# Idle products of 128x256 on TensorE behind steps of the two recurrences in the layers

## The chip, the cores and the metric

The kernel runs as one program on one core of a Trainium2 chip. TensorE (PE) multiplies matrices, VectorE (DVE), ScalarE (ACT) and GpSimd (POOL) do the element-wise work, and SyncE (SP) issues the transfers. The time is device microseconds of one launch. TensorE's clock has two levels, 2.4 and 1.2 GHz; the profile shows the granted clock as a share of the higher one, so 1.00 and 0.50.

## The reference, cut to what matters

The model is two blocks. The first has two layers of feed-forward, mixer, feed-forward. Its mixer runs three mechanisms on the same projected rows (sequence 512): a sparse attention that keeps 128 keys per query, chosen by a small indexer (`dsa`), an RWKV-7 recurrence (`rwkv`) and a gated delta rule (`delta`). The second block has a forgetting attention with a gated linear attention, a cross attention and a mixture of experts. The change touches the two recurrences of the first block alone. In the reference they are:

```
# rwkv7_scan, per step
sa = jnp.einsum('bhij,bhj->bhi', S, at)
S = S * wt[:, :, None, :] + sa[..., None] * bt[:, :, None, :] + vt[..., None] * kt[:, :, None, :]
y = jnp.einsum('bhij,bhj->bhi', S, rt)

# chunk_gated_delta_rule, per chunk
v_new = uc - jnp.einsum('bhck,bhkv->bhcv', wc, S)
o = jnp.einsum('bhck,bhkv->bhcv', qc * jnp.exp(gc)[..., None], S) + jnp.einsum('bhcs,bhsv->bhcv', ac, v_new)
S = S * jnp.exp(g_last)[..., None, None] + jnp.einsum('bhck,bhcv->bhkv', kc * jnp.exp(g_last[..., None] - gc)[..., None], v_new)
```

## The kernel before, in words

Both recurrences are computed in four chunks of 128 tokens, q = 0 to 3, four heads of width 64 each. Every chunk is a chain of small fp32 products with a copy out of PSUM between them.

- `rwkv_pe` (strand `r`) works in banks 0 and 1. For each q it makes the masked scores (AK, RB, RK; line 1107 through `scores`), then `wv` (1204, 1205), `sa` (1211: four products of 128x64), `y` (1223 to 1225) and `state` (1234, 1235). DVE copies between them: `wv` at 1428, `sa` at 1432, the state at 1439. Behind the last chunk come the means (1240: two products of 128x512).
- `delta_pe` (strand `d`) works in banks 2, 3 and 4 (`R.D4` is bank 4; its `B[0]` is bank 2). For each q: `rest` (1573), `vn` (1579), `delta_y` (1590, 1591) and `delta_state` (1601). DVE reads them at 1781, at 1788 and 1789, and at 1797.
- `dsa_pe` (strand `s`) works in banks 5 to 7: the indexer's products (1984) with ACT's relu (2027) and DVE's sum (2091), then DVE's choice of the keys, sixteen rounds of MAX8 and MATCH_REPLACE8 (2101, 2103), and then the attention: scores (1864), transposes (1873), values (1882).

Each engine's program is written out by `in_turns(TURNS, ...)`: a strand is a Python generator, each `yield` ends a step, and `TURNS` is a fixed list of letters that says whose step comes next. All four engines use the same list. Nothing is reordered at run time: on each engine the instructions run in the order written, and one that waits for a semaphore holds up all behind it.

A product signals its reader by `.then_inc` on the last instruction of its step, so a product written behind that one does not delay the signal; it stands ahead of whatever comes next on PE. An fp32 product is recorded as two matmuls in the profile, so a count of x8 is four products. The shapes in the rows are the stationary tile, and then output and input.

The kernel has idle products already, in `norm_pe`, whose result nobody reads:

```
for _ in range(2):
    e.matmul(bank[first][:, :], ones, C("cmask"), start=True, stop=True)
```

`ones` is a 128x128 constant of ones, and `C("cmask")` a constant of 128x512, of which the first 384 columns are zero.

Of the kernel before, what the change touches and what calls it, by code (L numbers as in the profile page):

```python
# [16 lines left out]
NT = SEQ // P  # L17
# [147 lines left out]
def build(nc, x_in, mem_in, const_in, w1_in, w2_in, y_out):  # L165
    with ExitStack() as ctx:
# [56 lines left out]
        def C(name, n=None):  # L223
            a, w = CONST[name]
            return const[:, a:a + w] if n is None else const[:, a + n * P:a + (n + 1) * P]
# [19 lines left out]
        ident, ones, bones = C("ident"), C("ones"), C("bones")  # L245
# [542 lines left out]

        def head_sum(stat, c, t):
            return stat[:, 2 * (c * NT + t):2 * (c * NT + t) + 2]

# [330 lines left out]
        def rwkv_pe(e, R):  # L1124
            l, B, W = R.l, R.B, R.W
# [4 lines left out]
            for c in range(2):  # L1130
                for n, (lo, hi) in enumerate(LORA):
                    if 3 * c + n >= 2:
                        e.wait_ge(*act.at("lora", l, 3 * c + n - 2))
                    e.matmul(B[(3 * c + n) % 2][:, :], up[lo:hi, c * P:(c + 1) * P], R.lora[lo:hi, :], start=True,
                             stop=True).then_inc(*pe.step(("up", l, 3 * c + n)))
# [54 lines left out]
            for q in range(NT):  # L1190
                for n, (lhs, rhs) in enumerate(((R.Kt, R.At), (R.Bt, R.Rt), (R.Kt, R.Rt))):
                    if n:
                        e.wait_ge(*dve.at(("AK", "RB")[n - 1], l, q))
                    else:
                        e.wait_ge(*(dve.at("state_raw", l, q - 1) if q else dve.at("T", tag, 6, NT - 1)))
                    scores(e, lhs, rhs, q, B).then_inc(*pe.step((("AK", "RB", "RK")[n], l, q)))
                    yield
                e.wait_ge(*dve.at("RK", l, q))
                e.wait_ge(*dve.at("scaled", l, q))
                for half in range(2):  # L1200
                    part = half_of(half)
                    for c in range(2):
                        h, o = 2 * half + c, B[half][:, c * HD:(c + 1) * HD]
                        e.matmul(o, R.At[part, cols_of(c, q)], R.scaled[part, c, :], start=True, stop=False)
                        made = e.matmul(o, R.AK[:, h, :], R.v_tok[:, q, c * P + half * HD:c * P + (half + 1) * HD],
                                        start=False, stop=True)
                    made.then_inc(*pe.step(("wv", l, q, half)))
                yield
                e.wait_ge(*dve.at("wv", l, q))
                for h in range(4):  # L1210
                    made = e.matmul(B[0][:, h * HD:(h + 1) * HD], R.Tt[:, q, h, :], R.wv[:, h, :], start=True, stop=True)
                made.then_inc(*pe.step(("sa", l, q)))
                yield
                e.wait_ge(*dve.at("sa", l, q))

                def vs(h):
                    return R.v_tok[:, q, (h % 2) * P + (h // 2) * HD:(h % 2) * P + (h // 2 + 1) * HD]

                for half in range(2):
                    part = half_of(half)  # L1220
                    for c in range(2):
                        h, o = 2 * half + c, B[half][part, c * P:(c + 1) * P]
                        e.matmul(o, R.scaled[part, c, :], R.Rt[part, cols_of(c, q)], start=True, stop=False)
                        e.matmul(o, R.sa[:, h, :], R.RB[:, h, :], start=False, stop=False)
                        made = e.matmul(o, vs(h), R.RK[:, h, :], start=False, stop=True)
                    made.then_inc(*pe.step(("y", l, q, half)))
                yield
                for half in range(2):
                    part = half_of(half)
                    e.wait_ge(*act.at("y", l, q, half))  # L1230
                    for c in range(2):
                        h, o = 2 * half + c, B[half][part, c * HD:(c + 1) * HD]
                        hs = slice(c * P + half * HD, c * P + (half + 1) * HD)
                        e.matmul(o, R.b_tok[:, q, hs], R.sa[:, h, :], start=True, stop=False)
                        made = e.matmul(o, R.k_tok[:, q, hs], vs(h), start=False, stop=True)
                    made.then_inc(*pe.step(("state", l, q, half)))
                yield
# [252 lines left out]
        def delta_pe(e, R):  # L1490
# [73 lines left out]
            for q in range(NT):  # L1564
                if q:
                    e.wait_ge(*dve.at("state", l, q - 1))
                else:
                    e.wait_ge(*dve.at("state0", l))
                    e.wait_ge(*act.at("q_decay", l, 1))
                for half in range(2):  # L1570
                    part = half_of(half)
                    for c in range(2):
                        made = e.matmul(B[half][:, c * HD:(c + 1) * HD], kf[part, cols_of(c, q)], R.state[part, c, :],
                                        start=True, stop=True)
                    made.then_inc(*pe.step(("rest", l, q, half)))
                yield
                e.wait_ge(*dve.at("rest", l, q))
                for h in range(4):
                    made = e.matmul(R.D4[:, h * HD:(h + 1) * HD], R.Tt[:, q, h, :], R.rest[:, h, :], start=True,
                                    stop=True)  # L1580
                made.then_inc(*pe.step(("vn", l, q)))
                yield
                e.wait_ge(*dve.at("vn", l, q))
                if q == 0:
                    e.wait_ge(*dve.at("q_decay", l, 1))
                for half in range(2):
                    part = half_of(half)
                    for c in range(2):
                        h, o = 2 * half + c, B[half][part, c * P:(c + 1) * P]
                        e.matmul(o, R.state[part, c, :], qf[part, cols_of(c, q)], start=True, stop=False)  # L1590
                        made = e.matmul(o, R.vn[:, h, :], R.Xt[:, q, h, :], start=False, stop=True)
                    made.then_inc(*pe.step(("delta_y", l, q, half)))
                yield
                e.wait_ge(*dve.at("vs", l, q))
                for half in range(2):
                    part = half_of(half)
                    e.wait_ge(*act.at("delta_y", l, q, half))
                    for c in range(2):
                        h, o = 2 * half + c, B[half][part, c * HD:(c + 1) * HD]
                        hs = slice(c * P + half * HD, c * P + (half + 1) * HD)  # L1600
                        made = e.matmul(o, R.k_tok[:, q, hs], R.vs[:, h, :], start=True, stop=True)
                    made.then_inc(*pe.step(("delta_state", l, q, half)))
                yield
            yield from heads_pe(e, ("o", l), W, R.stat, B, [dve.at("state", l, NT - 1)])
            yield
# [1866 lines left out]
```

## Time and profile before

| | |
|---|---|
| median of 3 runs | 3742.98 us (3742.59 to 3748.95) |
| profiled execution: its own time, its span | 3745.36 us, 3743.6 us |
| PE, PEld, DVE, ACT, POOL busy | 93%, 75%, 51%, 37%, 12% |
| mean granted clock | 0.941 |
| HBM traffic over the span | 110 GB/s |

The span is from the first to the last instruction of one profiled execution; the time of that execution is 1.76 us longer. Busy shares are averages over stages with quite different limits. In the chain that ended last, the costliest lines lie in the experts at the end of the program (L2925, 10% of the span). The mixers of the two layers lie between about 385 and 945 us and between about 1730 and 2290 us; their last parts, where the recurrences run beside the sparse attention, are from 780 and from 2125 us on.

### The profile page before, as it was taken

Reading aid. Unit: us, or ns where it says so; the run is one execution under the profiler, and the core shown is the slowest. Engines: PE = TensorE matmul, PEld = TensorE weight load, DVE = VectorE, ACT = ScalarE, POOL = GpSimd, SP = SyncE. Lnnn points to the kernel's source line nnn. Section 1 sums busy time; section 2 is a strip of 40 time slices with the busy share of each in tenths; the row PEclk is TensorE's granted clock in tenths of the full one; section 3 lists DMA queues with packets and bytes.
Section 4 is the critical chain, followed back from the end, with each engine's and each line's share of the span. In section 5 each row is a group of like instructions: output and inputs, shape, how many; then the busy total and the mean of one; then the engine's idle time right before and its main releaser. Section 6 shows DMA issues by size and latency. Waiting matters only on the chain. (4 is left out here: it accounts for less than half of the span.)

```text
span 3743.6 us, 43164 instructions
## 1 busy us (share of the span) xinstructions
PE 3494.3 (93%) x17900; PEld 2809.5 (75%) x17900; DVE 1913.4 (51%) x2897; ACT 1397.2 (37%) x1940; POOL 436.0 (12%) x217
## 2 busy tenths in 40 slices
PE   8999996998999999999997989999999998699995
PEld 6888786875788888887786856888777665578884
DVE  4343444675443444343626764434335333389995
ACT  3222443642321232123444524312244333277772
POOL 1000332000000000002321000000131000122222
PEclk9999998996999999999998969999998989799997
DMA  4443210000223222222100002222221211499994
GB/s 172 148 139 114 79 68 1 1 23 23 90 90 108 90 100 92 100 92 88 71 24 1 24 1 79 90 103 90 102 90 46 79 46 45 184 362 409 407 408 150
DMA packets 65986, 414.61 MB, mean 111 GB/s; under 512 B 6912, under 2 KB 11136, under 8 KB 22272
## 3 DMA queue, kind: packets, MB, share of 16 engines
q1 hardware_dynamic: 63488, 403.46, 28.8%
q0 software_dynamic: 2304, 8.39, 0.6%
q8 instruction: 142, 2.33, 0.3%
q14 instruction: 52, 0.43, 0.0%
HBM read 375.13 MB, written 36.70 MB: 110 GB/s over the span
## 5 line engine op out<-in xcount | busy, mean ns | idle before, releaser
L344 DVE TENSOR_TENSOR w_lo<-ring,w_hi 128x2048 fp32r<-128x2048 f32 x146 | 334.4, 2292 | 869.0 <-ACT w_hi L340 869.0
L340 ACT ACTIVATE w_hi<-ring 128x2048 fp32r<-128x2048 f32 x146 | 280.1, 1920 | 1001.9 <-PE bank L469 584.6
L469 PE MATMUL bank<-x_hi,w_lo 128*128 128x512 f32 x1344 | 533.5, 397 | 0.0
L469 PE MATMUL bank<-x_hi,w_hi 128*128 128x512 f32 x1344 | 527.3, 392 | 0.0
L469 PE MATMUL bank<-x_lo,w_hi 128*128 128x512 f32 x1344 | 524.2, 390 | 0.0
L469 PEld LDWEIGHTS bank<-x_lo,w_hi 128*128 128x128 f32 x1344 | 252.3, 188 | 62.2
L469 PEld LDWEIGHTS bank<-x_hi,w_lo 128*128 128x128 f32 x1344 | 252.3, 188 | 58.0
L469 PEld LDWEIGHTS bank<-x_hi,w_hi 128*128 128x128 f32 x1344 | 252.3, 188 | 54.5
L513 PE MATMUL bank<-h_hi,w_hi 128*128 128x512 f32 x704 | 274.0, 389 | 0.0
L513 PE MATMUL bank<-h_hi,w_lo 128*128 128x512 f32 x704 | 274.0, 389 | 0.0
L513 PE MATMUL bank<-h_lo,w_hi 128*128 128x512 f32 x704 | 273.8, 389 | 0.0
L372 POOL TENSOR_TENSOR tmp<-tmp 128x512 f32<-128x512 f32 x54 | 76.0, 1407 | 1182.9 <-ACT tmp L365 1176.4
L2906 ACT ACTIVATE e_hi<-arena 128x2048 fp32r<-128x2048 f32 x92 | 176.3, 1916 | 24.0 <-PE bank L2925 21.2
L2911 DVE TENSOR_TENSOR e_lo<-ring,e_hi 128x2048 fp32r<-128x2048 f32 x45 | 150.0, 3333 | 44.0 <-ACT e_hi L2906 44.0
L2911 DVE TENSOR_TENSOR e_lo<-arena,e_hi 128x2048 fp32r<-128x2048 f32 x70 | 157.6, 2276 | 6.1 <-ACT e_hi L2906 6.1
L513 PEld LDWEIGHTS bank<-h_hi,w_hi 128*128 128x128 f32 x704 | 132.2, 188 | 27.5
L513 PEld LDWEIGHTS bank<-h_lo,w_hi 128*128 128x128 f32 x704 | 132.2, 188 | 27.5
L513 PEld LDWEIGHTS bank<-h_hi,w_lo 128*128 128x128 f32 x704 | 132.2, 188 | 27.5
L703 PE MATMUL bank<-x_hi,ring_r 128*128 128x512 f32 x352 | 139.8, 397 | 0.0
L2916 POOL TENSOR_TENSOR e_lo<-arena,e_hi 128x2048 fp32r<-128x2048 f32 x22 | 101.8, 4625 | 318.3 <-ACT e_hi L2906 318.3
L998 POOL TENSOR_TENSOR ring_r<-ring,high 128x1024 fp32r<-128x1024 f32 x44 | 110.4, 2532 | 225.7 <-ACT high L990 225.7
L998 POOL TENSOR_TENSOR ring_r<-ring,first 128x1024 fp32r<-128x1024 f32 x6 | 14.3, 2405 | 1045.7 <-ACT first L990 1045.7
(562 smaller groups left out, 6988.2 us busy)
## 6 DMA issues: line engine op xcount, KB each, us to landing
ring<-slots SPq DMA_DIRECT2D x238, 1024.0 KB, 4.8
arena<-slots SPq DMA_DIRECT2D x92, 1024.0 KB, 8.4
x_rows<-v_first SPq DMA_DIRECT2D x23, 512.0 KB, 6.7
xn<-x_rows SPq DMA_DIRECT2D x23, 512.0 KB, 8.3
y_rows<-xn SPq DMA_DIRECT2D x23, 512.0 KB, 8.8
x_aside<-xT SPq DMA_DIRECT2D x3, 2048.0 KB, 6.3
xT<-x_aside SPq DMA_DIRECT2D x3, 2048.0 KB, 9.0
xT<-x_t SPq DMA_DIRECT2D x2, 1024.0 KB, 10.4
```

Of the source, the lines that this page charges most:

```text
L340: e.activation(w_hi[:, k % 2, :], ring[:, k % RING, :], ACT.Copy).then_inc(*act.step(("hi", k)))
L344: e.tensor_tensor(w_lo[:, k % 2, :], ring[:, k % RING, :], w_hi[:, k % 2, :].bitcast(F32), ALU.subtract).then_inc(*dve.step(("slot", k)))
L372: e.tensor_tensor(SUM[:, :], SUM[:, :], squares[i][:, :], ALU.add).then_inc(*pool.step(("sum", tag, i)))
L469: made = e.matmul(bank[b + f][:, :], w.rearrange("p (k n) -> p k n", k=KC)[:, c, f * P:(f + 1) * P], (x_hi, x_lo)[part][:, c, :], start=c ...
L513: made = e.matmul(bank[d][:, :], w.rearrange("p (f n) -> p f n", f=2)[:, f, d * P:(d + 1) * P], rows[part][:, 2 * n + f, :], start=n == 0 ...
L703: made = e.matmul(out, w[:, c0:c0 + P], x, start=i == 0 and m == 0, stop=i == KC - 1 and m == 2)
L998: e.tensor_tensor(half_slot(ring_r[:, k % RING, :], half), raw, half_slot(high_of(N, n), half).bitcast(F32), ALU.subtract).then_inc(*pool. ...
L2906: e.activation(e_hi[m % W_BUFS][:, :], e_ring[m % E_RING], ACT.Copy).then_inc(*act.step(("expert_hi", m)))
L2911: e.tensor_tensor(e_lo[m % W_BUFS][:, :], e_ring[m % E_RING], e_hi[m % W_BUFS][:, :].bitcast(F32), ALU.subtract).then_inc(*dve.step(("expe ...
L2916: e.tensor_tensor(e_lo[m % W_BUFS][:, :], e_ring[m % E_RING], e_hi[m % W_BUFS][:, :].bitcast(F32), ALU.subtract).then_inc(*pool.step(("exp ...
```

## The change: one product behind some steps

A helper is added, and is called behind four kinds of step. With q from 0 to 3 that makes 2 products (`sa`), 3 (`rest`), 4 (`vn`) and 3 (`delta_state`), so 12 in each layer and 24 in all. None has a wait or a signal of its own. Each writes 256 columns of a bank that its strand has read and that the strand's next use overwrites.

```diff
+        def idle_product(e, b):
+
+            e.matmul(b[:, 0:256], ones, C("cmask")[:, 0:256], start=True, stop=True)
+
@@ rwkv_pe
                 made.then_inc(*pe.step(("sa", l, q)))
+                if q >= 2:
+                    idle_product(e, B[1])
                 yield
@@ delta_pe
                     made.then_inc(*pe.step(("rest", l, q, half)))
+                if q:
+                    idle_product(e, R.D4)
                 yield
@@
                 made.then_inc(*pe.step(("vn", l, q)))
+                idle_product(e, B[0])
                 yield
@@
                     made.then_inc(*pe.step(("delta_state", l, q, half)))
+                if q < NT - 1:
+                    idle_product(e, R.D4)
                 yield
```

The order of all other instructions is the same on every engine. Line numbers move: a line of the strands stands 4 to 11 lines further down in the kernel after (1984 becomes 1995); L793 is the new product. Three places on PE follow, each of one layer.

The first is chunk q = 1 of `delta`, where `rest` (second half), the indexer's products and `vn` alternate. Before:

```order
L1573 MATMUL bank3<-arena 128x64 x2
L1984 MATMUL bank5<-arena 128x512
L1984 MATMUL bank6<-arena 128x512
L1579 MATMUL bank4<-arena,xn 128x64 x4
L1984 MATMUL bank5<-arena 128x512
L1984 MATMUL bank6<-arena 128x512
```

After, in the same place:

```order
L1579 MATMUL bank3<-arena 128x64 x2
L793 MATMUL bank4<-const 128x256
L1995 MATMUL bank5<-arena 128x512
L1995 MATMUL bank6<-arena 128x512
L1587 MATMUL bank4<-arena,xn 128x64 x4
L793 MATMUL bank2<-const 128x256
L1995 MATMUL bank5<-arena 128x512
L1995 MATMUL bank6<-arena 128x512
```

Two products stand ahead of the first and of the second pair of the indexer's products.

The second is chunk q = 2 of `rwkv`: the end of `wv`, `sa`, and the start of `y`. Before:

```order
L1204 MATMUL bank1<-arena,xT 128x64
L1205 MATMUL bank1<-arena 128x64
L1211 MATMUL bank0<-arena 128x64 x4
L1223 MATMUL bank0<-xT,arena 64x128
L1224 MATMUL bank0<-arena 64x128
```

After:

```order
L1208 MATMUL bank1<-arena,xT 128x64
L1209 MATMUL bank1<-arena 128x64
L1215 MATMUL bank0<-arena 128x64 x4
L793 MATMUL bank1<-const 128x256
L1229 MATMUL bank0<-xT,arena 64x128
L1230 MATMUL bank0<-arena 64x128
```

One product stands between `sa` and `y`; there is none ahead of `sa`, in `wv`.

The third is behind chunk q = 1 of `delta`, where its state step, the scores of the attention (L1864) and `rest` of q = 2 follow each other. Before:

```order
L1601 MATMUL bank3<-arena,xT 64x64 x2
L1864 MATMUL bank5<-arena 128x512
L1573 MATMUL bank2<-arena 128x64 x2
L1573 MATMUL bank3<-arena 128x64 x2
L1864 MATMUL bank5<-arena 128x512
```

After:

```order
L1610 MATMUL bank3<-arena,xT 64x64 x2
L793 MATMUL bank4<-const 128x256
L1875 MATMUL bank5<-arena 128x512
L1579 MATMUL bank2<-arena 128x64 x2
L1579 MATMUL bank3<-arena 128x64 x2
L793 MATMUL bank4<-const 128x256
L1875 MATMUL bank5<-arena 128x512
```

Each of the two scores has a product in front of it.

## Rows read from the trace of the kernel before

**Rows 1.** The page of the profile: span, section 1, and the granted clock by slice.

```profile
span 3743.6 us, 43164 instructions
...
PE 3494.3 (93%) x17900; PEld 2809.5 (75%) x17900; DVE 1913.4 (51%) x2897; ACT 1397.2 (37%) x1940; POOL 436.0 (12%) x217
...
PEclk9999998996999999999998969999998989799997
```

**Rows 2.** Windows view, both layers' slow stretches and the end of the first.

```profile
842.60:900.60 58.00, 47.90 (x193) 30.59 (x194) 40.24 (x99) 6.63 (x15) 0.00 (x0) 0.50 0.00 0
2187.40:2245.40 58.00, 47.90 (x194) 30.59 (x193) 40.24 (x99) 6.63 (x15) 0.00 (x0) 0.50 0.00 0
...
885.60:900.50 14.90, 14.85 (x46) 7.76 (x46) 6.94 (x26) 4.37 (x9) 0.00 (x0) 0.50 0.00 0
```

**Rows 3.** Windows view, two microseconds each, around the clock's fall and rise.

```profile
840.00:842.00 2.00, 2.00 (x12) 1.43 (x10) 1.69 (x3) 1.00 (x2) 0.00 (x0) 1.00 0.00 0
842.00:844.00 2.00, 1.62 (x9) 1.29 (x8) 1.18 (x4) 0.00 (x0) 0.00 (x0) 0.65 0.01 4
...
848.00:850.00 2.00, 2.00 (x9) 1.20 (x8) 1.93 (x4) 0.09 (x1) 0.00 (x0) 0.50 0.00 0
...
900.00:902.00 2.00, 2.00 (x9) 0.81 (x8) 0.69 (x1) 0.00 (x0) 0.00 (x0) 0.84 0.00 0
```

**Rows 4.** Timeline of PE, layer 0 (start, length, line, tiles, shape, count, idle before).

```profile
834.07 1.10 PE L1579 MATMUL bank<-arena,xn 128*128 128x64 f32 x8
835.10 1.23 PE L1984 MATMUL bank<-arena 64*128 64x512 f32 x4
...
839.68 0.33 PE L1204 MATMUL bank<-arena,xT 64*128 64x64 f32 x2
...
843.45 1.97 PE L1211 MATMUL bank<-arena 128*128 128x64 f32 x8 [0.38 <-DVE arena L1428]
846.49 0.68 PE L1223 MATMUL bank<-xT,arena 64*64 64x128 f32 x2 [1.07 <-DVE arena L1432]
...
876.83 0.68 PE L1223 MATMUL bank<-xT,arena 64*64 64x128 f32 x2 [1.40 <-DVE arena L1432]
...
885.65 2.07 PE L1864 MATMUL bank<-arena 64*128 64x512 f32 x2 [1.69 <-DVE arena L2124]
...
888.51 2.07 PE L1864 MATMUL bank<-arena 64*128 64x512 f32 x2
...
892.04 1.97 PE L1579 MATMUL bank<-arena,xn 128*128 128x64 f32 x8
...
896.80 3.78 PE L1240 MATMUL bank<-arena,const 128*128 128x512 f32 x4
```

**Rows 5.** Timeline of PE, first span: where the clock came back at 791.

```profile
786.39 3.73 PE L850 MATMUL bank<-ring 128*128 128x128 f32 x16
789.91 1.78 PE L859 MATMUL bank<-xn,tmp 128*128 128x128 f32 x8
```

**Rows 6.** Timeline of PE: the kernel's own idle products of 128x512.

```profile
383.39 1.45 PE L405 MATMUL bank<-const 128*128 128x512 f32 x3
```

**Rows 7.** Source view of that line: least, median and greatest length in ns.

```profile
L405 PE MATMUL bank<-const x12: 592/592/592, 383.4 to 2705.6; 128*128 128x512 f32 x12
```

**Rows 8.** Timeline of PE behind the slow stretch, layer 0.

```profile
907.38 0.66 PE L1873 MATMUL bank<-const,arena 128*128 128x128 f32 x4 [0.28 <-ACT arena L1923]
```

**Rows 9.** Timeline of DVE in the slow stretch, layer 0.

```profile
846.01 0.42 DVE L1432 COPY arena<-bank 128x256 f32<-128x256 f32 x1
...
853.32 0.28 DVE L1439 TENSOR_TENSOR arena<-arena,bank 64x128 f32<-64x128 f32 x1 [2.34 <-PE bank L1235]
854.82 0.29 DVE L1439 TENSOR_TENSOR arena<-arena,bank 64x128 f32<-64x128 f32 x1 [1.21 <-PE bank L1235]
...
860.93 0.76 DVE L1113 TENSOR_TENSOR arena<-bank,const 128x256 f32<-128x256 f32 x2 [3.85 <-PE bank L1107]
...
896.91 0.69 DVE L1908 CUSTOM_DVE_ANT_0 arena<-bank,arena 128x512 f32<-128x512 f32 x1 [2.03 <-PE bank L1864]
```

## The prediction, made before the result was known

> **What bounds the kernel now.** I read the page first. PE is busy for 93% of the span, but the granted clock by slice is not 9 everywhere: it dips where the mixers of the layers are [rows 1]. Since the change adds work to PE and removes none, it can only pay through that clock, so the next view was the windows view around the recurrences. Its columns are the stretch, its length, then busy time of PE, PE's weight loads, DVE, ACT and POOL, and then the granted clock. In each layer there is a stretch of 58 us, 842.6 to 900.6 and 2187.4 to 2245.4, in which the clock is at 0.50 throughout (1.2 GHz). The two are alike to the hundredth, so I work on the first and double it [rows 2].
>
> Then the finer windows, to see what PE did before the clock fell and before it rose [rows 3]. It fell at 842.6, and from 840 to 842 PE was busy for 2.00 of 2.00 us. So no idle time stands directly ahead of the fall. The timeline says what filled these microseconds: `wv`, sixteen products of only 64 columns, from 839.68 on [rows 4]. The clock stayed low through `y`, where PE is busy without a break (848 to 850), and it came back at 900.6. Ahead of that stand four full matmuls of 128x512 that took 3.78 us from 896.80 on. The same was seen at 791, where `wv` and `sa` of q = 1 were followed by 16 and 8 matmuls of 128x128, 3.73 and 1.78 us long, in a row [rows 5]. Both times about four to five microseconds of work on the full 128x128 tile brought the clock back.
>
> Last, who waits in the slow stretch. Up to 885 DVE is the busier side. It chooses the keys, and PE waits for it before `y` of q = 2 (1.07 us), before `y` of q = 3 (1.40) and before the first scores (1.69) [rows 4]. But DVE also waits for PE, 2.34, 1.21 and 3.85 us around `state` and `delta_y` of the slow clock [rows 9]. From 885.6 to 900.5 PE is busy for 14.85 of 14.90 us and the others wait for it [rows 2, 9].
>
> **The change part by part.** It adds 24 products of 128x256, 12 in each layer. The price of one is from the kernel's own idle products. Three recorded matmuls of 128x512 take 1.45 us, and one alone 592 ns, so they start (1450 - 592) / 2 = 429 ns apart [rows 6, 7]. A product of 512 columns is two such matmuls, so one of 256 columns costs 0.43 us at full clock. At half clock four such matmuls took 3.78 us, 0.94 each, and a product of 256 columns costs 0.94 [rows 4]. In the order of the layer:
>
> 1. Four at full clock ahead of the fall: behind `vn` and `delta_state` of q = 0, and behind `rest` and `vn` of q = 1. PE has no gap there: `vn` at 834.07 plus 1.10 us meets the indexer's products at 835.10 [rows 4]. The last two stand ahead of indexer products, from which ACT's relu, DVE's sum and the whole choice of keys hang in a chain, so a delay of PE goes straight into DVE. On the path: 4 x 0.43 = 1.72 us.
> 2. Behind `sa` of q = 2, behind `sa` of q = 3, and behind `delta_state` of q = 1: these fill the waits of 1.07, 1.40 and 1.69 us, each longer than 0.94 [rows 4]. What hides them is DVE's choice of keys; DVE reaches its copy of `sa` at 846.01 straight from that work, with no wait for PE [rows 9]. Cost 0. Without the cover they would cost 3 x 0.94.
> 3. Behind `rest` and `vn` of q = 2, at half clock, in the stretch where PE has no gap. Behind the first stand the scores of 888.51, and DVE and ACT wait for those; behind the second stand the transposes and then the scores for which DVE waits 2.03 us [rows 4, 9]. On the path: 2 x 0.94 = 1.88 us.
> 4. Behind `delta_state` of q = 2 and `rest` and `vn` of q = 3, at full clock again. One wait of PE of 0.28 us behind `rest` takes up a part [rows 8]: 3 x 0.43 - 0.28 = 1.01 us.
>
> That is 1.72 + 1.88 + 1.01 = 4.6 us a layer and 9.2 us for both, if the clock stays as it is.
>
> The products are not seen in their places before, so both sides. From below each costs nothing, if its time disappears in a wait further on that the trace puts down elsewhere: 0 us. From above each also pays a weight load that nothing covers. A product of 64 columns in `vn` takes 1.10 / 4 = 0.27 us at full clock and 1.97 / 4 = 0.49 at half, nearly all of it such overhead [rows 4]; seven times 0.27 and twice 0.49 add 2.9 us a layer, so 15 us in all. I take the middle value, because the kernel's own idle products run 429 ns apart with their weight loads hidden.
>
> Now the clock. Does it still fall at `wv` of q = 2? I say yes. No product is inserted in `wv` or ahead of `sa`; the nearest one before stands ahead of the indexer products of 835.10, 4.6 us before `wv` starts [rows 4], and the nearest one after comes when `sa` is done. Between them the row of small products is what it was. Does it come back sooner? One product gives 0.94 us of full-tile work, where the two rises of this trace had 3.78 and 5.5 us of it in a row [rows 4, 5]. The closest the change comes to that is behind `vn` of q = 2: a product, transposes, scores of 64 rows, and then the same four matmuls as before. So I leave the clock's pattern as it is. The moment of the fall can shift by a microsecond or two against the program, since everything ahead of it runs 1.7 us later; at half against full clock that is worth below 1 us a layer with either sign.
>
> [...] The fall at 842.6 with PE busy throughout speaks against busy time alone as the measure.
>
> The sum against the profiled execution is 3745.36 + 9.2 = 3754.6. That execution is 2.4 us above the median of the runs shown, so against the median it is 3742.98 + 9.2 = 3752.2. I predict 3752.
>
> **The rivals.** A, the clock holds: from `sa` of q = 2 on it stays at 1.00, in both layers. For it: five of the twelve products stand within the slow stretch, three of them in the very waits of PE. Against: the fall with PE busy, and nothing added in `wv`. What it gives: of the 7.4 us that DVE waits (2.34 + 1.21 + 3.85) I take half, 3.7. In the 14.9 us at the end, `vn` goes from 1.97 to 1.10 us, a ratio of 0.56, so 6.6 us are saved. That is 10.3 a layer. The products cost 9 x 0.43 - 0.28 = 3.6 then. Net -6.7 a layer, 3742.98 - 13.4 = 3729.6. It decides from the point where the windows around 846 show 1.00. This is the rival on the other side, faster than before.
>
> B, the clock comes back early, behind `delta_state` of q = 1. There `y` and both state steps end in a dense run, and the new product lengthens it by 0.94 us ahead of the scores of 885.65. Then the last 14.9 us run at full clock: -6.6, products 3.6, net -3.0 a layer and 3737.0 for both. In one layer alone: -3.0 + 4.6, so 3744.6. For it: this is the densest run with a product behind it. Against: `y` and the state step use tiles of half the rows or half the columns, and at half clock they never brought a rise by themselves [rows 3].
>
> C, the products are hidden in places where I put them on the path, because ACT and DVE set the pace of the attention between 832 and 842 and behind 901. Half the price of parts 1 and 4: 1.4 us a layer less, and 3749.5; if part 3 is hidden too, 3745.7. For it: PE does wait for ACT there, 0.28 us [rows 8]. Against: these waits are far shorter than a product.
>
> D, the change doesn't do what it says: the moving operand is all zeros, and such products may not count as activity at all. The time is that of the forecast, 3752; only the windows with products in them would tell it apart.
>
> **How the numbers follow.** The forecast with D: 0.62. C: 0.14. B: 0.12, shared between one and both layers. A: 0.12. About 0.2%, 7.5 us, is what a measurement of this kernel can tell from no change. Of the forecast's 0.62 some 0.45 lies above 3750.5, and 0.17 between that and the median, since the bounds 0 and 15 us and the shift of the moments at which the clock changes spread it. C is within 0.2%. Of B half a case is: one layer is within 0.2%, both layers are just within it or below, 0.05 faster. A is faster. So faster 0.17, same 0.38, slower 0.45. The forecast's own range is 3746 to 3758. The range for 8 in 10 takes in C and B and leaves out A below, and above it stops at the upper bound of the price: 3737 to 3758.
>
> **What would show it.** Right: 48 matmul records of the new line, 214 ns of streaming each at full clock; a clock of 0.50 still from about 844 to 905, longer by the two products of part 3; the waits before `y` of q = 2 and q = 3 gone or nearly gone with `y` no later against DVE's copy; the indexer's first products 1.3 us later than before and its second pair 1.7. Wrong: a clock of 1.00 anywhere between 846 and 896 (A or B); a length from 832 to the end of the mixer that has grown by less than 3 us with the same clock (C); a slow stretch in a stage that the change doesn't touch.

## The result and the profile after

The changed kernel took 3758.75 us (median of 6 runs), 14.9 us more than before beside it (3743.89): a ratio of 1.0044, with a 95% interval of 1.0028 to 1.0061. Measured again in one session with experiments, it took 3758.06 against 3744.87, 1.0036 [1.0023, 1.0049]. It is slower, as predicted, but by 13 to 15 us and not by 9.

The page of the kernel after, against [rows 1]:

```profile
span 3757.8 us, 43260 instructions
...
PE 3513.2 (93%) x17948; PEld 2821.4 (75%) x17948; DVE 1914.0 (51%) x2897; ACT 1397.2 (37%) x1940; POOL 435.4 (12%) x217
...
PEclk9999998996999999999998978999998988699997
```

48 matmuls more (an fp32 product of 256 columns is two), 18.9 us more of busy PE, and the same picture of the clock but for single slices. The windows view after, in answer to [rows 2, 3]:

```profile
845.20:847.20 2.00, 1.61 (x11) 1.36 (x10) 1.30 (x5) 0.00 (x0) 0.00 (x0) 0.89 0.01 4
847.20:905.20 58.00, 51.07 (x197) 31.69 (x196) 39.21 (x97) 6.64 (x15) 0.00 (x0) 0.50 0.00 1
2202.30:2260.30 58.00, 51.13 (x197) 31.80 (x196) 39.25 (x97) 6.64 (x15) 0.00 (x0) 0.50 0.00 1
```

The mean of 0.89 in the first row puts the fall at 846.8, 4.1 us later than before; the second came 14.4 us later (2201.85 against 2187.47). The clock stayed at 0.50 for the same 58.0 us. (The windows shown here and below, from other traces than that of before, start 0.1 to 0.7 us behind the fall.) PE is busy for 51.1 of them in place of 47.9: three gaps were filled or shortened, and the length of the slow stretch did not change. The timeline of PE after, at the places of [rows 4]; L793 is the new product:

```profile
824.78 0.65 PE L793 MATMUL bank<-const 128*128 128x256 f32 x2
825.27 0.49 PE L1884 MATMUL bank<-const,arena 128*128 128x128 f32 x3
...
835.02 0.70 PE L793 MATMUL bank<-const 128*128 128x256 f32 x2
835.65 1.13 PE L1995 MATMUL bank<-arena 64*128 64x512 f32 x4
...
847.92 1.17 PE L793 MATMUL bank<-const 128*128 128x256 f32 x2
849.46 0.69 PE L1229 MATMUL bank<-xT,arena 64*64 64x128 f32 x2 [0.38 <-DVE arena L1438]
...
888.63 2.07 PE L1875 MATMUL bank<-arena 64*128 64x512 f32 x2 [0.53 <-DVE arena L2135]
...
891.55 1.22 PE L793 MATMUL bank<-const 128*128 128x256 f32 x2
892.70 2.07 PE L1875 MATMUL bank<-arena 64*128 64x512 f32 x2
...
897.99 1.17 PE L793 MATMUL bank<-const 128*128 128x256 f32 x2
898.95 1.06 PE L1884 MATMUL bank<-const,arena 128*128 128x128 f32 x4
```

The price of a product is the distance from its start to the next start: 825.27 - 824.78 = 0.49 us where a full tile follows, 835.65 - 835.02 = 0.63 where a tile of 64 rows follows (0.59 at 837.65, behind `vn` of q = 1); at half clock 898.95 - 897.99 = 0.96 and 892.70 - 891.55 = 1.15. The wait before `y` of q = 2 shrank from 1.07 to 0.38 us, that before the scores from 1.69 to 0.53.

Where did the 14.2 us between the two spans arise? DVE passes four marks that both programs have: its work behind `state` of q = 1 in each layer (just ahead of the first product), and its first splitting of weights behind each mixer. Before:

```profile
823.03 0.59 DVE L1439 TENSOR_TENSOR arena<-arena,bank 64x128 f32<-64x128 f32 x2
...
961.97 2.29 DVE L344 TENSOR_TENSOR w_lo<-ring,w_hi 128x2048 fp32r<-128x2048 f32 x1 [12.68 <-ACT w_hi L340]
...
2167.88 0.60 DVE L1439 TENSOR_TENSOR arena<-arena,bank 64x128 f32<-64x128 f32 x2
...
2306.80 2.29 DVE L344 TENSOR_TENSOR w_lo<-ring,w_hi 128x2048 fp32r<-128x2048 f32 x1 [12.65 <-ACT w_hi L340]
```

And after:

```profile
823.73 0.59 DVE L1445 TENSOR_TENSOR arena<-arena,bank 64x128 f32<-64x128 f32 x2
...
967.87 2.29 DVE L344 TENSOR_TENSOR w_lo<-ring,w_hi 128x2048 fp32r<-128x2048 f32 x1 [11.19 <-ACT w_hi L340]
...
2178.88 0.59 DVE L1445 TENSOR_TENSOR arena<-arena,bank 64x128 f32<-64x128 f32 x2
...
2322.95 2.29 DVE L344 TENSOR_TENSOR w_lo<-ring,w_hi 128x2048 fp32r<-128x2048 f32 x1 [11.16 <-ACT w_hi L340]
```

By differences, the first layer's part took 138.94 us and now 144.14, the second's 138.92 and now 144.07: 5.2 a layer. But the stretch between them, in which no product stands, went from 1205.91 to 1211.01: 5.1 us more. I call these three lengths the parts of a trace; before they are 138.9, 1205.9, 138.9. The rest of the 14.2 us lies outside them: 0.7 us more ahead of the first mark, and 2.0 less behind the last one (3757.8 - 2322.95 against 3743.6 - 2306.80), in the second block.

The extra in the middle is the clock. The windows view after shows it at half speed at places of the program where the trace of before has it at full speed, with PE busy throughout:

```profile
1758.50:1761.90 3.40, 3.40 (x10) 2.62 (x10) 0.00 (x0) 1.40 (x2) 0.20 (x1) 0.55 0.40 164
1901.90:1905.30 3.40, 3.40 (x19) 3.40 (x19) 0.25 (x1) 2.00 (x2) 1.39 (x1) 0.56 0.10 39
1942.40:1945.80 3.40, 3.40 (x32) 3.16 (x32) 1.77 (x3) 0.00 (x0) 0.00 (x0) 0.50 0.00 0
```

The third of these falls has a counterpart before, but in another place of the program, some 5 us of work earlier, where DVE is idle for 2.98 us until a result of POOL:

```profile
1928.10:1931.50 3.40, 3.40 (x17) 3.40 (x17) 0.42 (x2) 0.86 (x2) 3.01 (x2) 0.50 0.00 0
```

By the starts of the same instructions on DVE in both traces, 1.6, 1.6 and 1.7 us are lost at the three places: 4.9 of the 5.1.

### The profile page after: what moved, and what is told of

It is laid out like the page before. It is cut to its first block and busy times, and to the rows that moved or that the text cites. A ratio compares the mean times of both kernels' runs of the same rounds, so it can differ in the third digit from the quotient of the medians.

```text
span 3757.8 us, 43260 instructions
## 1 busy us (share of the span) xinstructions
PE 3513.2 (93%) x17948; PEld 2821.4 (75%) x17948; DVE 1914.0 (51%) x2897; ACT 1397.2 (37%) x1940; POOL 435.4 (12%) x217
## 5 line engine op out<-in xcount | busy, mean ns | idle before, releaser
L1002 POOL TENSOR_TENSOR ring_r<-ring,first 128x1024 fp32r<-128x1024 f32 x6 | 14.4, 2417 | 1047.1 <-ACT first L994 1047.1
```

Of the source, the lines that this page charges most:

```text
L1002: e.tensor_tensor(half_slot(ring_r[:, k % RING, :], half), raw, half_slot(high_of(N, n), half).bitcast(F32), ALU.subtract).then_inc(*pool. ...
```

## The experiments

Theory 1 says that the loss is the local price of the products. Theory 2 adds that the delay moves the program against the moments at which the clock changes, so that stages without a product change too. Before took 3744.3 to 3744.9 us in each of the four sessions; each result is a median, with the ratio to before in the same session and its interval. That interval is 7 to 18 us from end to end, so differences of 2 or 3 us are read from the parts of the one trace of each kernel and not from the medians. The places behind the last mark hold no product in any of the kernels, and yet that stretch took from 3.5 us less (`e1_layer0`) to 24.0 us more (`e4_scores7`) than before.

**The parts of the change.** Products in the first layer only (`q >= 2 and l == 0` and so on at each place):

> All twelve products in the first layer, none in the second. Theory 1, local price: each product costs 0.49 to 0.63 us at full clock and 0.96 to 1.15 at half where nothing hides it (the starts of the next instruction in the trace after), which is 5.3 us in this layer and nothing elsewhere: 3743.9 + 5.3 = 3749.2. Theory 2, moments of the clock: the later program also meets the clock's changes otherwise in stages without a product; between 960 and 1935 us of the trace after another 4 to 5 us were lost where nothing was added. If the delay of the first layer is enough for that, 3753.5.

3750.3 us, 1.0013 [0.9999, 1.0028]; parts 144.1, 1207.6, 138.9. The local 5.2 us are there, and 1.7 in the middle; behind the last mark the trace is 3.5 us shorter than before. The second layer only:

> All twelve products of the second layer, none in the first. Theory 1: 5.2 us on top of before, 3749.6, like the first layer alone (3750.3). Theory 2: nothing is delayed ahead of the second layer, so only the stages behind it can shift; the part that the two layers together have beyond 2 x 5.3 (4 to 5 us) should then be missing here as it was with the first layer alone, 3748 to 3751, and only both layers together show it. A result of 3753 or more would say that the second layer's products cost more than the first layer's and would fit neither.

3749.2 us, 1.0007 [0.9994, 1.0020]; parts 138.9, 1206.0, 144.1: again 5.2, and 0.1 in the middle. Only the products in PE's waits:

```
-                if q:
-                    idle_product(e, R.D4)
...
-                idle_product(e, B[0])
...
-                if q < NT - 1:
+                if q == 1:
                     idle_product(e, R.D4)
```

> Only the three products of each layer that fill a wait of PE: behind sa of q = 2 and q = 3 and behind delta_state of q = 1. Theory 1: nothing, 3743.9 (within 1 us). Theory 2 gives the same, since nothing is delayed. If the products bring the clock back before the last 15 us of the slow stretch, 6.6 us less a layer.

3745.3 us, 1.0006 [0.9996, 1.0015]; parts 138.9, 1205.9, 138.9, within 0.02 us of those of before. Its windows:

```profile
841.40:899.40 58.00, 51.05 (x200) 32.00 (x200) 40.73 (x100) 6.63 (x15) 0.00 (x0) 0.50 0.00 0
2186.30:2244.30 58.00, 51.06 (x200) 31.97 (x200) 40.73 (x100) 6.64 (x15) 0.00 (x0) 0.50 0.00 1
```

PE is busy 51.05 us in place of 47.90 [rows 2], with no cost in the parts and no effect on the length of the slow stretch. Only the seven at full clock (`vn` of q = 0, 1, 3, `delta_state` of q = 0, 2, `rest` of q = 1, 3), and only the two behind `rest` and `vn` of q = 2:

> Only the seven products of each layer that run at full clock: behind vn of q = 0, 1, 3, behind delta_state of q = 0, 2, behind rest of q = 1, 3. Theory 1: 0.49 + 0.63 + 0.63 + 0.59 ahead of the fall and about 1.5 behind the rise, 3.8 a layer: 3751.6. As I predicted (0.43 each): 3743.9 + 5.5 = 3749.4. Theory 2: 3751.6 and up to 5 more.

> Only the two products of each layer at half clock behind rest and vn of q = 2. Theory 1: 1.15 + 0.96 a layer, 3743.9 + 4.2 = 3748.1. As I predicted (0.94 each): 3747.7. Theory 2: up to 5 more.

3751.9 us, 1.0023 [1.0012, 1.0035], parts 142.6, 1201.2, 143.3; and 3751.3, 1.0028 [1.0004, 1.0053], parts 140.4, 1206.2, 140.8. So the seven cost 3.6 and 4.4 us, 0.52 to 0.63 each, and the two 1.4 and 1.9. The first median is what theory 1 expected (3751.6), the second is 3 us above its 3748.1, with a wide interval. The middle is 4.7 us shorter in the first and 0.3 longer in the second: it varies by more than the products cost. The trace of the second also has a stretch of 44 us at half clock in the second block, far from any product:

```profile
3002.40:3046.80 44.40, 43.33 (x124) 25.57 (x125) 8.63 (x28) 11.81 (x26) 0.00 (x0) 0.50 0.00 0
```

**The whole again.**

> The changed kernel itself, unaltered, timed again beside the others. Two theories of why it took about 15 us more and not 9. Theory 1, local price: each product costs 0.49 to 0.63 us at full clock and about 1.0 to 1.15 at half, 5.3 us a layer, 10.6 in all; the rest of the 15 was the accident of the few runs it was measured with. It expects 3744.4 + 10.6 = 3755.0. Theory 2, moments of the clock: the delay moves the clock's short falls against the program in stages that hold no product, for 4 to 5 us more in most runs. It expects 3759.

3758.1 us; parts 144.1, 1207.7, 145.6: 5.2 + 1.8 + 6.7 = 13.7 us, and the median is 13.2 above before. This is the same kernel as in the first measurement, whose parts gained 5.2, 5.1 and 5.2 us and whose last stretch lost 2.0: the two traces come out 14.2 and 14.1 us longer than before, with the loss in different places. The two layers alone cost 5.9 and 4.4 by the medians, in sum 10.2. The 3 us between that and 13.2 are within the intervals; in the traces, the second layer's part is 1.5 longer here than with its products alone, with 3.4 us more of half clock behind the slow stretch.

**What a product is made of.** The moving operand from the table of rotations, `C("rope")[:, 0:256]`:

> The changed kernel with the 256 columns of the moving operand taken from the table of rotations, which is not zero, in place of the mask's zeros. If products with zeros do not count as activity (rival D of the prediction), then these should hold or bring back the clock where the zeros did not: the slow stretches shorter than 58.0 us, and up to 13 us less than the changed kernel. If the operand's values do not matter: 58.0 us again in both layers, and the time of the changed kernel within 2 us.

3758.2 us, parts 144.2, 1207.7, 145.6, and 58.0 us of half clock in both layers: the same as zeros. By itself this says only that one product in a place does nothing with either operand. But the three in a row that bring the clock back below are zeros too, so zeros do count, and rival D falls. The stationary tile of 64 rows, `ones[0:HD, :]`:

> The changed kernel with the idle product on a stationary tile of 64 rows in place of 128. If the part of the price over 0.43 us is a switch between products of 64 and of 128 rows (0.14 to 0.2 us in the trace, where the neighbour has 64 rows): behind vn, delta_state and rest the next product has 64 rows too in most places, so the gap should go from 0.63 to 0.43 to 0.5 us there, and the whole from 3758 to 3755 to 3757. If it is not a switch of rows: 0.49 to 0.63 again and 3758.

3752.9 us, 1.0017 [1.0001, 1.0033]; parts 144.0, 1207.6, 140.8. The timeline of PE, of the same places as above:

```profile
823.61 0.70 PE L793 MATMUL bank<-const 64*128 64x256 f32 x2
824.24 0.55 PE L1885 MATMUL bank<-const,arena 128*128 128x128 f32 x3
...
889.85 1.16 PE L793 MATMUL bank<-const 64*128 64x256 f32 x2
890.81 1.91 PE L1876 MATMUL bank<-arena 64*128 64x512 f32 x2
...
833.94 0.43 PE L793 MATMUL bank<-const 64*128 64x256 f32 x1
833.96 0.69 PE L1996 MATMUL bank<-arena 64*128 64x512 f32 x1
```

The prices changed places: behind `vn` of q = 0 and 3, where a full tile follows, 0.63 us (0.49 with 128 rows); at half clock 0.96 (1.15) where 64 rows follow. So a change in the number of rows costs 0.14 us at full and 0.19 at half clock in these places, as expected. It isn't the whole of it: behind `delta_state` of q = 0 a tile of 128 rows and 64 columns follows, and the price is 0.63 with either product. And in the last two rows the product of 64 rows and the indexer's first matmul start 0.02 us apart: from `rest` to `vn` of q = 1 it takes 1.61 us before, 2.28 with the product of 128 rows and 1.93 with that of 64. The first layer's part hardly moved, though: three products behind `vn` (q = 0, 2, 3) got dearer by 0.14 to 0.19, and those with 64 rows behind them cheaper. The second's 3.3 us less come with 10.2 us of half clock behind the slow stretch in place of the 17.1 of the trace shown first, not with the price.

**More products: can the clock be held?** 17 in each layer: within both halves of `wv` of q = 2 and 3, behind `sa`, behind the scores of q = 3 in the delta strand's free bank, and three behind `delta_state` of q = 1; none behind `rest` and `vn`:

```
+                    if q == 3:                        # behind each scores(...) of AK, RB, RK
+                        filler(e, bank[4], 2 + (n == 2))
...
+                        if c and q >= 2:              # wv
+                            filler(e, B[half])
...
+                if q >= 2:                            # sa
+                    filler(e, B[1], q - 1)
...
+                if q == 1:                            # delta_state
+                    for _ in range(3):
+                        idle_product(e, R.D4)
```

> Does the clock stay up if the idle products stand where the small steps themselves are, and not only behind them? None behind rest and vn; 17 in each layer: one within each half of wv of q = 2 and 3, one behind sa of q = 2, two behind sa of q = 3, two, two and three behind the score products of q = 3 into the delta strand's free bank, three behind delta_state of q = 1. If this keeps the clock (the windows from 846 to 896 at 1.00): the slow stretch gives back 10.3 us a layer by the working of rival A, and four products in wv cost 4 x 0.43 = 1.7, the others lie in PE's waits of 0.87 to 2.46 us: 8.6 a layer less, 3727. If more full products do not keep it: 58 us at 0.50 again, and at half clock the four in wv cost 3.8, those behind the scores 1.88 - 0.87, 1.88 - 1.40 and 2.82 - 2.46 = 1.9 over the waits, those behind sa 0.5 and behind delta_state 1.1: about 7.3 a layer more, 3759. Both theories on the price say the same here; what it tells apart is whether filling the gaps failed for the place of the products or for good.

3737.7 us, 0.9977 [0.9968, 0.9987], between the two cases; parts 135.4, 1206.0, 133.9. Its windows:

```profile
847.20:860.90 13.70, 13.24 (x65) 8.25 (x63) 7.28 (x20) 1.33 (x4) 0.00 (x0) 0.51 0.01 1
860.90:867.70 6.80, 5.44 (x32) 3.89 (x30) 6.46 (x14) 0.00 (x0) 0.00 (x0) 0.99 0.00 0
867.70:884.80 17.10, 16.72 (x61) 11.47 (x60) 15.28 (x33) 0.76 (x2) 0.00 (x0) 0.51 0.00 0
884.80:899.70 14.90, 14.54 (x93) 8.39 (x92) 8.26 (x29) 7.48 (x16) 0.00 (x0) 1.00 0.01 1
```

The slow stretch is cut in pieces, 31 us in place of 58. The clock came back behind the products at the scores and behind the three at `delta_state`. Each place by itself:

> Only three products behind delta_state of q = 1 in each layer, nothing else: what rival B of the prediction needs, with more of it. In the kernel with products also behind the scores the clock stood at 0.50 up to 884.8 and at 1.00 behind these three (2.83 us of them). If the three alone bring it back: the slow stretch ends near 885 instead of 900.6, which gives 6.6 us a layer, and the three cost 2.83 - 1.69 = 1.1 us over the wait that they fill: 5.5 us a layer less, 3733 to 3735. If they only did it with the products ahead of them: 58 us again, and 1.1 us a layer more, 3747.

3732.8 us, 0.9964 [0.9948, 0.9980]; parts 133.7, 1211.2, 133.7: 5.2 us less a layer, for three products. The middle is 5.2 us longer in this trace, which is one of the slowest executions of the kernel (3738.3 us); the median is 11.6 below before, so most executions don't have that.

```profile
842.60:887.00 44.40, 35.97 (x153) 24.71 (x153) 34.27 (x77) 2.27 (x6) 0.00 (x0) 0.50 0.00 0
887.00:901.90 14.90, 14.33 (x93) 8.27 (x92) 8.61 (x32) 7.68 (x17) 0.00 (x0) 1.00 0.01 1
```

The clock fell at 842.3 (842.6 before), and rose at 886.7, not at 900.6. The timeline of PE shows what stands there:

```profile
883.68 2.93 PE L793 MATMUL bank<-const 128*128 128x256 f32 x6
886.54 1.19 PE L1871 MATMUL bank<-arena 64*128 64x512 f32 x2
```

Three products in a row, 2.86 us at half clock, and the scores behind them start at half and end at full speed. Two in their place:

> Two products behind delta_state of q = 1 in each layer, nothing else. One left the slow stretch at 58.0 us, three cut it to 44.4. If it turns between one and two: 44.4 us, the two cost 1.88 - 1.69 = 0.2 us over the wait they fill, so 6.4 us a layer less than before, 3731.6, a microsecond a layer better than three. If two are too few: 58.0 and 3745.

3745.4 us, 1.0011 [0.9990, 1.0032], with runs from 3736 to 3772, five of the twelve between 3736 and 3740; parts 139.0, 1207.5, 133.9. One trace holds both outcomes, the first layer without and the second with the gain:

```profile
841.60:899.60 58.00, 49.79 (x198) 31.76 (x198) 40.50 (x100) 6.63 (x15) 0.00 (x0) 0.51 0.00 0
2189.90:2230.90 41.00, 32.80 (x141) 22.13 (x142) 31.84 (x73) 2.27 (x6) 0.00 (x0) 0.51 0.00 0
```

The same instructions, and once they brought the clock back and once not. One did not in any layer; three with nothing else beside them did in both. The seven behind the scores alone:

> Only the seven behind the score products of q = 3 in each layer, none behind delta_state. If any row of full products between half-used tiles brings the clock back: it rises near 861 to 863 as with the ten, falls again at 870 in wv, and then stays low to 900, since nothing is behind delta_state: 7 us of low clock less in a stretch in which PE waits for DVE, worth 2 to 3.5 us a layer, less about 0.4 us by which the products run over the waits: 3738 to 3741. If the two places only work together: 58 us and 3746 to 3748.

3751.5 us, 1.0025 [1.0012, 1.0039]; parts 137.3, 1207.7, 138.8. A miss: the clock did rise at 860.5, for 6.8 us in which PE waits for DVE anyway, and fell again for 30.7 us. That is worth 1.6 and 0.2 us, not 2 to 3.5; and this trace has 64.9 us of half clock in the second block. That the median is 7 us above before can't come from the layers, whose parts shrank; the middle (1.8) and the stretch behind the last mark are what grew, and 4 of the 12 runs stand at 3766 to 3770. The scores and `delta_state` together:

> The three behind delta_state of q = 1 and the seven behind the score products of q = 3, none in wv and none behind sa. If wv's four and sa's three did nothing for the clock but bring the fall from 842 to 847: it falls near 842, rises near 861 behind the scores, falls again in wv of q = 3 and rises at 885; against the kernel with 17 products about 5 us more of low clock in each layer (some 2 us of time) and 4 x 0.43 = 1.7 us less of products on the path: within 1 us a layer of it, 3736 to 3739. If the rise at 861 needed them: like the three alone plus 1.9 us a layer for products at half clock.

**3728.4 us, 0.9959 [0.9941, 0.9976], the fastest of all, 16 us below before and 30 below the changed kernel.** Parts 130.3, 1207.8, 130.3: 8.6 us less a layer, where the three and the seven alone had 5.2 and at most 1.6. Expected was 3736 to 3739; the products in `wv` and behind `sa` had cost more than they brought.

```profile
843.00:863.50 20.50, 18.59 (x85) 11.96 (x84) 12.46 (x30) 1.52 (x4) 0.00 (x0) 0.51 0.00 1
863.50:870.30 6.80, 5.43 (x32) 4.00 (x30) 6.53 (x15) 0.00 (x0) 0.00 (x0) 0.97 0.00 0
870.30:887.40 17.10, 14.57 (x54) 10.23 (x55) 15.26 (x34) 0.76 (x2) 0.00 (x0) 0.51 0.00 0
887.40:902.30 14.90, 14.33 (x95) 8.34 (x93) 8.96 (x34) 8.04 (x17) 0.00 (x0) 1.00 0.01 1
```

26 products a layer, two in each half of `wv` of q = 3, three behind `sa`, one in each half of `y`:

> The 17 products of the faster kernel, and 9 more a layer: a second one in each half of wv of q = 3, three behind sa of q = 2 and q = 3, one within each half of y of q = 2 and q = 3. If they hold the clock where it still fell (847.2 for 13.7 us, 867.7 for 17.1): windows at 1.00 from 836 to 896, about 31 us of half clock less a layer, of which DVE's own work hides a part; taken at a third, 10 us, less 6 x 0.43 + 1.0 = 3.6 on the path: 4 to 6 us a layer less than the kernel with 17, 3726 to 3730. If the stretches stay: 26 products cost 3.6 to 7 us a layer more than 17, 3745 to 3751.

3737.2 us, 0.9979 [0.9959, 1.0000]; parts 133.7, 1207.8, 137.0. The clock was held up to 868, and then fell at other places:

```profile
836.00:868.00 32.00, 27.61 (x159) 17.54 (x159) 25.85 (x57) 5.00 (x11) 0.00 (x0) 0.99 0.00 1
868.00:878.20 10.20, 9.82 (x32) 7.11 (x32) 7.68 (x19) 0.00 (x0) 0.00 (x0) 0.52 0.00 0
...
888.40:898.60 10.20, 10.20 (x32) 5.21 (x29) 4.19 (x15) 2.98 (x7) 0.00 (x0) 0.52 0.00 0
```

20 us of half clock in the place of 58, and yet 9 us slower than the kernel with 38 (20.5 + 17.1). My reading, not tested further: what counts is the stretch where PE sets the pace, from 885 to 900, in which this kernel fell back to half clock, and the six products on the path in `wv` and four in `y`. The changed kernel with three in place of one behind `delta_state` of q = 1:

> The changed kernel with three products in place of one behind delta_state of q = 1. If its loss is price plus an unchanged slow stretch, then bringing the clock back at 885 should return 6.6 us a layer, less 1.1 for the two more, and the products behind rest and vn of q = 2 now cost 0.55 in place of 1.05 each: 6.5 a layer, 3758 - 13 = 3745, as fast as before. If the other products spoil the rise: 58 us and 3760.

3756.7 us, 1.0031 [1.0010, 1.0052], from 3739 to 3772 over 8 runs; parts 146.0, 1201.3, 136.9. Missed: half clock for 61.4 us in the first layer, for 41.0 in the second. With the other products around them, three no longer bring the clock back every time. Why, these runs don't show.

**A plain delay.** Before, with eight in place of two of its own idle products at the norm ahead of the second mixer:

```
-                for _ in range(2):
+                for _ in range(8 if tag == ("mix", 1) else 2):
```

> The kernel before, with no product in the recurrences, and six more of its own idle products of 128x512 at the norm ahead of the second layer's mixer (from 1728 us on): a plain delay of 6 x 0.86 = 5.15 us, as much as the twelve products of the first layer cost. Theory 1, local price alone: 5.15 us and nothing else, 3744.5 + 5.15 = 3749.7, and the stages behind keep their lengths. Theory 2, moments of the clock: the delay moves the program against the moments at which the clock can change, so the stretch from 1740 to 2168, which holds no added product, gets 1.8 to 5.1 us longer, as it did in every trace with the first layer's twelve products; 3751.5 to 3755.

3747.9 us, 1.0014 [1.0001, 1.0027]. In the trace the delay is 4.9 us: the next work of PE starts 6.86 us behind the first idle product in place of 1.96. The median grew by 3.6, where theory 2 expected 7 us or more. The profiled execution was one of the two slowest (3763 us), with the middle part 15.0 us longer, 4.9 of it the delay, the second layer's part 5.8 longer, and half clock where no other trace here has it:

```profile
2160.60:2198.10 37.50, 37.50 (x165) 25.00 (x165) 8.79 (x36) 9.69 (x24) 0.00 (x0) 0.50 0.00 1
```

So the clock's falls can land elsewhere in stages without an added product. Most executions of this kernel don't pay for it (nine of eleven are at 3746 to 3750 us), so as a rule that a delay costs extra, theory 2 isn't borne out; the interval, 0.4 to 10 us, doesn't exclude it.

## Why the prediction was wrong in size

**Right.** The step that the clock falls around `wv` of q = 2 all the same and comes back no sooner: 58.0 us twice, and the prediction's "behind `vn` of q = 2: a product, transposes, scores" changed nothing. The fall stands some 1.2 us later against the program, as it allowed for: 0.8 ahead of the start of `sa` before (842.6 and 843.45), 0.3 behind it after (846.8 and 846.43). The "sixteen products" of `wv` are eight, recorded as sixteen matmuls; nothing hangs on it. Part 2, the three products in PE's waits, priced at 0: shown, 138.94 us with and without them. Part 3, forecast 1.88 us: 1.15 + 0.96 = 2.11 by the starts, 1.4 to 1.9 by the kernel with these two alone. Rival A did not come. Rival C was true in a small part: by the starts the three parts on the path make 2.34 + 2.11 + 1.66 - 0.28 = 5.8 us, and the layer grew by 5.2. Rival D, with the time of the forecast, is refuted: zeros brought the clock back.

**Mis-sized: the price at full clock.** The working took 429 ns from idle products in a row. Between small steps a product costs 0.49 to 0.63: part 1 is 0.49 + 0.63 + 0.63 + 0.59 = 2.34, not 1.72. What the upper bound had charged as a weight load that nothing hides, at 0.27 us each, is 0.06 to 0.20; how much of that is the weight load isn't shown, and 0.14 of it goes with the number of rows. That makes 5.2 us a layer in place of 4.6, 1.1 us of the 4 to 6 that were missing.

**The step that failed** is the sentence that the clock's shift "is worth below 1 us a layer with either sign". It looked at the slow stretch alone. There it held. But the rest of the program was put at nothing, and there the clock's short falls landed in other places: in the four traces with the first layer's twelve products of 128 rows the middle took 1.7, 1.8, 1.8 and 5.1 us more. In the three kernels whose first layer took as long as before, it took 0.0, 0.1 and 1.5 more; and where that layer changed by other amounts, anything from 4.7 less to 5.2 more. The second layer's part took 1.5 us more than the price in two of the three traces with products in both layers. For the first profiled execution the sum closes: it was forecast at 3754.6 us and took 3759.57, and the 5.0 us between them are 1.1 of price, 5.1 in the middle, 0.7 ahead of the first product, less 2.0 behind the last mark. That the delay by the products is what moved the falls is argued, not shown: the same kernel lost 5.1 us in the middle once and 1.8 the other time. Why the medians of the changed kernel stay 3 to 4.5 us above the price of its products, while the delay at the norm cost no more than its length, stays open. "A slow stretch in a stage that the change doesn't touch" stood in the list of what would make it wrong, without a price; it was the term to price, from the short falls that the granted clock by slice showed all over the program [rows 1].

**Rival B was judged well for one product and too lightly for the idea.** The prediction gave the reason, that half-used tiles bring no rise, and took one product of 0.94 us as too little against 3.8 to 5.5 us in a row [rows 4, 5]. Three, 2.9 us, were enough where nothing else was added (with the other products around them they failed in one layer of two), and the 6.6 us that it worked out for the last 14.9 at full clock, less 1.1 for the two that don't fit the wait, is the 5.2 measured, within 0.3. On idle gaps (the Trainium skill, TensorE: Matmul & The Clock Gate, "Why this matters for your kernels") the page's rule is about gaps longer than any filled here (1.07, 1.40 and 1.69 us), so it did not promise that filling these would keep the clock. No run here tests that rule. What the runs add is that filling all three with one product each left 58.0 us of half clock, and that one of these places filled with three cut it to 44.4.

## What to carry to other kernels

In this kernel it paid to put idle products in a row, several at one place that a wait covers, just ahead of the stretch in which PE sets the pace; spread singly between small steps they cost their price and left the slow stretch as long as it was. Ten at four places of a layer gave 16 us, three at one place 12, and twelve at twelve places lost 13 to 15. More is not better: with 26 a layer the gain was 7, and three in a row with eleven others around them gave no gain over the changed kernel that eight runs could show. One trace doesn't price a small change in such a program: compare the stages that it doesn't touch, and expect some microseconds of either sign there.

## What the runs showed of the hardware beyond this

- The same instructions can have two outcomes: two products behind `delta_state` left 58.0 us of half clock in one layer and 41.0 in the next, in one execution.
- The clock can miss its rise for long in a stage that is as before: 44.4 us at half speed with PE busy for 43.33 of them, where the trace of before has short falls (6.8 us at 3003). It was seen in three traces, whose stretch behind the last mark took 14.0 to 15.4 us more than before. The kernel before has executions of 3757 to 3773 us too, of which no trace was kept.
- The time of the middle part, with the same instructions, was between 1201.2 and 1211.2 us over the seventeen traces in which nothing is added to it.
- The values of the operand (zeros or not) changed neither the clock nor the time (3758.2 against 3758.1).
- Between two full tiles, an idle product of 64 rows starts the next one 0.14 us later than one of 128 at full clock (0.63 against 0.49) and 0.19 later at half (1.15 against 0.96).
- PE busy is not enough for the full clock: at 0.50 it was busy for 14.85 of 14.90 us before [rows 2], and for 37.50 of 37.50 in the trace with the delay.
